# Turning and adding the halves of the 64 further tokens in two rounds of an expert layer, and gathering a ninth round's rows in that round

## What is computed

```python
def moe_ffn(x, router_w, w1, w3, w2):
    logits = xt @ router_w
    top_v, top_i = lax.top_k(logits, 2)
    top_w = softmax(top_v)
    gates = sum(one_hot(top_i, 8) * top_w[..., None], axis=1)
    for e in range(8):
        y = y + gates[:, e:e + 1] * ((silu(xt @ w1[e]) * (xt @ w3[e])) @ w2[e])
```

## Time and profile before

| | us |
|---|---|
| median of 3 runs | 2330.93 (2329.65 to 2336.23) |
| the profiled execution | 2330.9 |
| its span, first to last instruction | 2329.1 |
| PE busy | 2288.7 (98%) |
| DVE busy | 1810.3 (78%) |
| ACT busy | 1383.6 (59%) |

### The profile page before, as it was taken

The page is one execution under the profiler, slowest core; times in us unless marked ns, Lnnn a source line. Parts: engine busy times, 40 slices in busy tenths (PEclk is TensorE's granted clock), DMA queues, the critical chain, the costliest instruction groups (busy, mean ns, idle before and its releaser), DMA issues.

```text
span 2329.1 us, 29393 instructions
## 1 busy us (share of the span) xinstructions
PE 2288.7 (98%) x11211; PEld 1899.5 (82%) x11211; DVE 1810.3 (78%) x2342; ACT 1383.6 (59%) x1588; POOL 31.7 (1%) x44
## 2 busy tenths in 40 slices
PE   9999999999999999999999998999999999999998
PEld 7788887888888888787888877888888888888887
DVE  4865467989867687899899998899765569987655
ACT  4444444578755666788878874565544435654543
POOL 0000000000000000000000000000000000000000
PEclk9999999999999999999999999999999999999999
DMA  8366654699967799899999995644566565455663
GB/s 279 114 210 188 186 162 158 261 326 407 376 230 269 269 323 344 321 409 412 409 374 408 413 413 202 192 138 152 183 190 190 181 203 163 118 180 172 198 187 122
DMA packets 198508, 584.20 MB, mean 251 GB/s; under 512 B 17259, under 2 KB 26615, under 8 KB 183640
## 3 DMA queue, kind: packets, MB, share of 16 engines
q1 hardware_dynamic: 196060, 573.97, 70.1%
q0 software_dynamic: 1872, 6.82, 0.9%
q10 hardware_dynamic: 428, 1.45, 0.2%
HBM read 580.07 MB, written 2.12 MB: 250 GB/s over the span
## 4 chain that ended last, share of the span: by engine, by line
PE 88%; DVE 8%; ACT 1%; issue 1%; DMA 1%; DVEq 0%; POOL 0%; POOLq 0%; ACTq 0%; SPq 0%
PE tile L1005 19%; PE tile L1007 19%; PE tile L1006 19%; PE tile L1506 5%; PE tile L1507 5%; PE aux L1128 3%; DVE units_parts L2495 3%; PE aux L1492 2%; PE aux L1005 2%; PE aux L1006 2%; PE aux L1007 2%; PE aux L1507 1%; PE aux L1506 1%; PE aux L1419 1%; PE aux L1782 1%
## 5 line engine op out<-in xcount | busy, mean ns | idle before, releaser
L2495 DVE TENSOR_TENSOR units_parts<-units,high 128x1024 fp32r<-128x1024 f32 (+3 forms) x339 | 482.5, 1441 | 93.4 <-ACT high L1910 91.1
L1006 PE MATMUL tile<-units_parts,acts 128*128 128x512 f32 (+2 forms) x1344 | 515.0, 383 | 0.0
L1910 ACT ACTIVATE high<-units 128x1024 fp32r<-128x1024 f32 (+3 forms) x339 | 412.2, 1235 | 153.2 <-DMA units<-in_w_in 40.9
L1005 PE MATMUL tile<-high,acts 128*128 128x512 f32 (+2 forms) x1012 | 401.8, 397 | 6.5 <-DVE units_parts L2495 3.9
L1007 PE MATMUL tile<-high,acts 128*128 128x512 f32 (+2 forms) x1012 | 389.6, 385 | 0.0
L1006 PEld LDWEIGHTS tile<-units_parts,acts 128*128 128x128 f32 x1344 | 254.3, 189 | 47.1 <-issue 2.2
L1005 PEld LDWEIGHTS tile<-high,acts 128*128 128x128 f32 x1012 | 191.3, 189 | 44.9 <-DVE units_parts L2495 5.9
L1007 PEld LDWEIGHTS tile<-high,acts 128*128 128x128 f32 x1012 | 190.9, 189 | 38.5
L1006 PE MATMUL tile<-units_parts,zbuf_parts 128*128 128x512 f32 x328 | 127.6, 389 | 0.0
L1506 PE MATMUL tile<-high,params_parts 128*128 128x512 f32 x276 | 109.0, 395 | 0.0
L1507 PE MATMUL tile<-units_parts,params_parts 128*128 128x512 f32 x276 | 107.7, 390 | 0.0
(11 more groups left out here) (554 smaller groups left out, 5201.0 us busy)
## 6 DMA issues: line engine op xcount, KB each, us to landing
units<-in_moe_w SPq DMA_DIRECT2D x156, 1024.0 KB, 8.0
units<-in_w_in SPq DMA_DIRECT2D x134, 512.0 KB, 4.0
units<-in_w_ff SPq DMA_DIRECT2D x128, 512.0 KB, 3.7
q_buf<-in_moe_w SPq DMA_DIRECT2D x39, 1024.0 KB, 8.5
k_buf<-in_moe_w SPq DMA_DIRECT2D x39, 1024.0 KB, 8.2
nat<-in_moe_w SPq DMA_DIRECT2D x39, 1024.0 KB, 8.7
bias<-in_moe_w SPq DMA_DIRECT2D x39, 1024.0 KB, 9.0
units<-in_ffn_w SPq DMA_DIRECT2D x48, 512.0 KB, 3.7
```

The source lines that it names most:

```text
L1005: nc.tensor.matmul(bank, lhs[0], high, start=start, stop=False)
L1006: nc.tensor.matmul(bank, lhs[0], low, start=False, stop=False)
L1910: nc.scalar.activation(high_slot(SG[0], n) if wide_ else high_slot(SG[0], n)[:, 0:cols], halves(weights) if wide_ else weights[:, 0:cols], ...
L2495: V.tensor_tensor(low, weights, high, ALU.subtract).then_inc(SG[0].low_ready, 1)
```

## The change

Rounds 2 and 3 no longer fold. PE transposes the 8 blocks of a tile's raw products (`turn_raw`) into two spare banks, one for each matrix; DVE reduces each bank over its two halves (`add_halves`), ACT takes the silu in SBUF, DVE multiplies. In `LARGE` this comes one unit behind the turn (units 4t+6), in round 3 the second tile of a pair comes one unit behind the first (9 and 10, 17 and 18, 25 and 26). Rounds 5, 7 and above still fold. Round 7 no longer gathers for round 8: a ninth round would choose and gather for itself. The scatter in `second_matrix` moves from back units 2 and 3 to 4 and 6, and the choice in round 0 from unit 17 to 15.

```diff
-BACK_SCATTER, BACK_CHOOSE, BACK_GATHER = (2, 3), 2, (4, 5, 6, 7, 8, 9, 10, 11)
+BACK_SCATTER = (4, 6)
...
-    return r <= LARGE or few(r) and r < ROUNDS - 1
+    return r <= LARGE or few(r) and r != N_EXP - 1
...
+    return [r] if r >= N_EXP else [r + 1] if r <= LARGE else [r + 1, r + 2]
...
+def adds_up(r):
+
+    return r in (LARGE, LARGE + 1)
+
+
+def added_after(r, i):
+
+    if r == LARGE:
+        return [i // 4 - 1] if i >= 6 and i % 4 == 2 else []
+    return [i // 4 - 2 + i % 8 - 1] if r == LARGE + 1 and i >= 9 and i % 8 in (1, 2) else []
...
+def tail_added_at(r):
+
+    return TAIL_AT + (r == LARGE) if adds_up(r) else None
...
+                    def turn_raw(r, t):
+
+                        raws_of(r, t)
+                        for m in range(2):
+                            bank = spare_bank("raw", r, t, m)
+                            for c in range(4):
+                                at = slice(c * P, (c + 1) * P)
+                                mm = nc.tensor.transpose(bank[:, at], raw_of(r, t, m)[:, at], ident)
                             mm.then_inc(spare_full, 1)
...
                             for t in turned_after(r, i):
                                 turn_tile(r, t)
+                            for t in added_after(r, i):
+                                turn_raw(r, t)
                             if i in GATHER_AT and gathers_within(r):
                                 gather(r, GATHER_AT.index(i))
...
-                            if k in BACK_GATHER and gathers(r):
-                                gather(r, BACK_GATHER.index(k))
...
+                            for k in range(8):
+                                gather(s - 1, k)
                             first_matrices(s - 1, None, s - 2)
...
+                    def silu_added(r, t):
+
+                        n = spare_at["raw", r, t, 0]
+                        act.wait_ge(spare_evac[n % 2], n // 2 + 1)
+                        nc.scalar.activation(product_of(r, t)[0], product_of(r, t)[0], ACT.Silu).then_inc(few_silu, 1)
...
+                            if r == LARGE and i % 4 == 2:
+                                raw_out(r, i // 4, 0, 2)
...
-                            if r == LARGE and i % 4 == 1:
-                                raw_out(r, i // 4, 0, 2)
...
+            def add_halves(r, t):
+
+                banks = [spare_in("raw", r, t, m) for m in range(2)]
+                for (bank, evacuated_), dst in zip(banks, product_of(r, t)):
+                    V.tensor_reduce(dst, bank[:, :].rearrange("p (c i n) -> p c n i", c=4, i=2), AX.X,
+                                    ALU.add).then_inc(evacuated_, 1)
+                n = spare_at["raw", r, t, 1]
+                dve.wait_ge(spare_evac[n % 2], n // 2 + 1)
+                dve.wait_ge(few_silu, C.folded.take() + 1)
+                silu, linear = product_of(r, t)
+                V.tensor_tensor(silu, silu, linear, ALU.mult).then_inc(few_added, 1)
...
-                    if i == CHOOSE_AT + (4 if r == 0 else 0) and gathers_within(r):
+                    if i == CHOOSE_AT + (2 if r == 0 else 0) and gathers_within(r):
                         choose(gathered_lots(r), rank)
...
-                    if k == BACK_CHOOSE and gathers(r):
-                        choose(gathered_lots(r), rank)
```

More of the change, by code:

```diff
@@ L236, in gathers @@
 def gathers(r):
-    return r <= LARGE or few(r) and r < ROUNDS - 1
+    return r <= LARGE or few(r) and r != N_EXP - 1
 def gathered_by(r):
-    return [r + 1, r + 2] if LARGE < r < N_EXP - 1 and gathers(r) else [r + 1] if gathers(r) else []
+    if not gathers(r):
+        return []
+    return [r] if r >= N_EXP else [r + 1] if r <= LARGE else [r + 1, r + 2]
 def few(r):
@@ L1594, in first_matrices @@
                             if i == 0:
-                                for q in range(r):
+                                for q in range(r + 1):
                                     if r in gathered_by(q):
@@ L1603, in first_matrices @@
                                 turn_tile(back, LAST_TILE)
+                            if back is not None and i == tail_added_at(back):
+                                turn_raw(back, LAST_TILE)
                             if i in scatter_at(r) and late is not None:
@@ L2174, in first_matrices @@
                                 tile_in(back, LAST_TILE)
-                            if i == TAIL_AT + 2 and back is not None and (few(back) or back == LARGE):
+                            if back is not None and i == tail_added_at(back):
+                                silu_added(back, LAST_TILE)
+                            if i == tail_low_at(back):
                                 high_few(back, LAST_TILE)
@@ L2233, in expert @@
                             END[0] = C.unit.n + MOE_UNITS
+                            for k in range(8):
+                                gathered_in(s - 1, k)
                             first_matrices(s - 1, None, s - 2)
@@ L3075, in low_few @@
                 high, low = hidden_few(r, t)
-                V.tensor_tensor(low, product_of(r, t), high, ALU.subtract).then_inc(few_low, 1)
+                V.tensor_tensor(low, product_of(r, t)[0], high, ALU.subtract).then_inc(few_low, 1)
             def back_low(r):
@@ L3112, in first_matrices @@
                         tile_in(back, LAST_TILE)
-                    if i == TAIL_AT + 2 and back is not None and (few(back) or back == LARGE):
+                    if back is not None and i == tail_added_at(back):
+                        add_halves(back, LAST_TILE)
+                    if i == tail_low_at(back):
                         low_few(back, LAST_TILE)
@@ L3118, in first_matrices @@
                         tile_in(r, t)
+                    for t in added_after(r, i):
+                        add_halves(r, t)
                     if few(r):
```

51 lines of the change are left out of this document (35 added, 16 removed).

## The result

The changed kernel takes 2341.2 us, the median of 20 runs (2332.6 to 2350.6), against 2333.0 us of the kernel before in 20 runs beside it (2327.9 to 2337.6). The ratio is 1.0032, with a 95% interval of 1.0021 to 1.0044: 8 us slower, about the 0.3% that a measurement can tell from no change. The forecast was +3 us, with 2316 to 2341 us as its range; on its base of 2330.9 us the measured +8.2 us makes 2339.1. The profiled execution of after took 2340.7 us.

What follows compares the result with a forecast made beforehand. PE was taken to set the pace up to about 990 us, with transfers behind it following PE. The terms summed to -0.4 us, +3.0 with the clock, on 2330.9 us: 2334 us, range 2316 to 2341.

Steps and rivals of the forecast that it cites:

- rival (b): Five gathers of rounds 2 and 3: each wait lowers the clock and reductions take 0.8 us; 2340 us, chance 0.22.
- What bounds the kernel: Steps 2 and 3: PE sets the pace up to about 990 us; its gains or losses there move the end equally.
- Rival (c): Steps 2 and 3 do not matter, since transfers pace all that follows; 2328 us, chance 0.08.
- Rival (a): Rounds 2 and 3: DVE frees the banks in time, so no waits, late splits or clock loss; 2317 us, chance 0.25.
- Rival (d): Ninth round: none runs, so that part does not do what it says; included in every case, no chance of its own.
- Folds and insertions: PE, rounds 2 and 3: 14 tiles stop folding, -12.0 us; 10 more insertions among large matmuls, +1.0 us.
- late splits behind the first pair: Round 3: splits that come late behind the first pair of tiles, +0.5 us.
- VectorE's reductions: DVE, rounds 2 and 3: 0.60 to 0.65 us each, 0.81 at most; 21 us added in all, hidden as throughput.
- Banks that come free late: Five gathers, units 18, 22, 26 (round 2) and 18, 26 (round 3), wait for DVE's first reduction: +7.2 and +5.9 us.
- The clock: Behind the five new gather waits: two clock falls of 1.7 us each, +3.4 us, with 0 and 8.5 as ends.
- Round 0: First gather waits less for the selection matrix with the choice two units earlier, still waiting for DVE's subtractions: -0.5 us.
- Step 8: End of kernel: eight gathers leave PE, DVE then paces the end, PE ends a unit behind: -2.3 us.

Runs made afterwards that it cites:

- the variants: Changed kernel with gathers moved to units without raw transposes (2321.1 us), with gathers ahead of raw transposes (2321.3 us), or with both (2320.0 us).
- double reductions: Each of the 28 reductions done twice on DVE: 2353.0 us on the changed kernel, 2323.9 us on the changed kernel with gathers moved to units without raw transposes.
- filled waits: Changed kernel with PE repeating the second matrix's transposes at the five gather units, 12 more in round 2, 20 in round 3: 2336.9 us.

## Why the forecast was right, and where its terms were off

The measured +8.2 us lies in the range, but 1 us above the part of it that belonged to the forecast (2329 to 2338), and nearer to rival (b)'s 2340 us than to the sum's 2334. By the number alone (b) would be as good. What the forecast had right is the mechanism; what it had too small is the clock.

**What bounds the kernel** held. From the gates of round 4 to the last scatter the change and all nine experiments take 441.8 to 443.0 us, whatever the stretch ahead took (289.0 to 322.8), so each microsecond of steps 2 and 3 reached the end. Rival (c) falls. Rival (a), no waits and 2317 us, is what the variants nearly reach with 2320 to 2321. Rival (d) holds: no ninth round ran (the gates stand eight times in the trace, once a round).

**Folds and insertions**: 0.86 and 0.1 us close the sum in all kernels without double reductions. One detail was misplaced and cost nothing: the first tile's share lies ahead of the gates of round 2, and shows there as 132.1 to 131.3 us. The 0.2 us for a late bank at unit 21 of round 2 was a misreading: the trace of before lists no wait of PE there. The 0.5 us for late splits behind the first pair measured 0.4 (two waits of 0.2).

**VectorE's reductions** take 0.68 us, not 0.60 to 0.65; the row that reads PSUM was the right neighbour, and 0.81 was too high. They are hidden as throughput but for the places where PE needs their banks, as the doubled ones show.

**Banks that come free late** was the deciding step and it held at all five places with the releaser named: 14.2 us for 13.1 forecast. Round 2's three took 2.3 to 2.4 each, as worked out; round 3's took 3.4 and 3.8 for 2.7 and 3.2. From ACT's copy at 893.83 to the end of the first reduction at 897.96 + 0.68 = 898.64 are the 4.8 us of the step, but PE was done with its transposes 1.6 us behind the copy's start (895.39), not 2.1, and the gather came 0.15 behind the reduction. Turning round the order in the unit, and nothing else, takes the waits away.

**The clock** is the term that was mis-sized. I forecast two falls of 1.7 us each, 3.4. There were two, as many as I took, but of 6.8 us, worth 5.7 in the records and 5.3 in the experiment with filled waits. My price came from one fall, of 3.4 us, behind a wait of 1.6 us, and that others last 6.8 us it could not show. The runs beside the profile say more. Their mean granted clock is 0.9914 over the 20 runs of after, and 0.9952 over the 57 runs of the kernel before that stand beside the experiments. What the clock lacks to 1, times the span, is 20.1 and 11.2 us lost, so 8.9 us more (an upper figure, since it also counts low clock while PE stood, 2.2 us of the two falls in the profile). The means of the times, 2340.3 and 2332.7, differ by 7.6. So the clock's part is as large as the whole loss, and all other terms together come to about nothing, as the -0.4 of the sum had it. Rival (b), a fall behind each wait, is not what the profile of the change shows; it is what happened once the waits were 0.7 us longer. Its 8.5 us for the clock come near what the runs lost, but by luck, from five falls at half the length; and its reductions of 0.8 us took 0.68.

**Round 0** got 2.1 us shorter where I had -0.5. Some 0.4 of it is the shorter wait, now for DVE's subtraction as worked out; 1.7 is the clock: before had a fall of 3.4 us at 493.4 us behind its wait of 1.6 us, after waited 1.2 us and had none. Nor had any of the nine experiments, which all choose earlier and wait 1.1 to 1.2 us. Against them stands a single profile of before, so that the shorter wait prevents the fall is likely and not shown.

**Step 8** gave 1.8 us in the profile of after and 2.3 to 3.0 in those of the nine experiments, for 2.3. By how it was worked out it was half right: PE now starts its last matmul 1.8 us behind DVE's last split, as worked out, where it was 3.4 before; but the 0.6 us on DVE did not come. DVE's last split ends 439.2 us behind the gates of round 4 (987.8) and 439.3 before, so it gained 0.1, and PE's last matmul starts 441.0 us behind them and 442.7 before. Where the last transfer lands I did not follow up.

**What stays open.** The stretches of the two profiles differ by 4.8 us without the first row, and the clock fall of before at 493 us would make it 6.5; the medians differ by 8.2. The remaining 2 to 3 us fit falls in other executions, by the granted clocks above: the runs of after lie between 2332.6 us and 2350.6, their clocks between 0.994 and 0.987, the faster with the higher. Which stretches of those executions had them is not in one profile.

## What to carry to other kernels

Before an operation is moved from one engine to another, look at who frees the buffer that it uses, and what stands behind it in the same unit. Here 12 us of matmuls were saved and 14 us of waits and 6 us of clock came back, and swapping two calls in the order of PE and of ACT kept the saving. Put the consumer that needs a free bank ahead of the producer that fills both. And price a new stop of TensorE at its length plus what the clock may take behind it, which here was 1.7 or some 3 us more for each stop that brought a fall.

## What the runs showed of the hardware

Whether the clock falls behind a stop isn't settled by the stop's length in this case: three stops of 2.3 to 2.4 us brought no fall in one kernel and one fall in another, and one of 2.1 us brought one of 3.4 us; behind the ten of 2.8 to 4.4 us in the stretch of the folds there was one each time, of 3.4 or 6.8 us. Repeating useless transposes during the stop kept the clock at 1.00 and made the kernel 4 us faster than standing still (5.3 us in the stretch of the folds). Eight fp32 transposes of 128x128 take 0.87 us on PE and do there what 16 fold instructions did in 1.73; a reduction of 512 fp32 columns from PSUM to 256 takes 0.68 us on DVE. Executions of one kernel differ by up to 18 us, and falls of the clock of 3.4 to 13.7 us at places that have nothing to do with the change go with it: a change of 0.3% is read better by stretches between instructions that both kernels have than by the spans.
